# Second block's attention: index keys and queries projected first, index sums and selection beside the other projections, query roots as scale of the exponentials

## The reference

```python
    q = _rope(_rmsnorm(q, q_norm_g), positions)
    k = _rope(_rmsnorm(k, k_norm_g), positions)
    qi = _rope(qi, positions)
    ki = _rope(_layernorm(ki, idx_k_ln_g, idx_k_ln_b)[:, :, None, :], positions)[:, :, 0, :]
    ...
        s = jnp.einsum('bqhd,bsd->bqhs', qib, ki)
        score = jnp.einsum('bqhs,bqh->bqs', jax.nn.relu(s), wib).astype(jnp.float32)
        score = jnp.where(causal[None], score, -jnp.inf)
        _, sel = lax.top_k(score, topk)
        ...
        logits = jnp.einsum('bqgrd,bqkgd->bqgrk', qg, kg).astype(jnp.float32) * scale
        logits = jnp.where(sel_ok[:, :, None, None, :], logits, -1e30)
        p = jax.nn.softmax(logits, axis=-1).astype(vg.dtype)
```

## Time and profile before

| | us |
|---|---|
| median of 3 runs | 1908.45 (1906.66 to 1910.44) |
| the profiled execution, its own time | 1910.37 |
| its span, first to last instruction | 1908.6 |
| TensorE busy in the span | 1756.0 (92%) |
| VectorE busy | 1068.7 (56%) |
| ScalarE busy | 734.9 (39%) |
| GpSimd busy, 12 instructions | 12.0 (1%) |

### The profile page before, as it was taken

One profiled execution on the slowest core, in us unless ns is written; L12 is line 12 of the kernel. 1 busy time (PEld: TensorE's weight loads), 2 busy tenths in 40 slices (PEclk: granted clock), 3 DMA queues, 4 the chain that ended last, 5 costly groups with the idle time before them and its releaser, 6 DMA issues.

```text
span 1908.6 us, 22987 instructions
## 1 busy us (share of the span) xinstructions
PE 1756.0 (92%) x7616; PEld 1352.9 (71%) x7616; DVE 1068.7 (56%) x2153; ACT 734.9 (39%) x1406; POOL 12.0 (1%) x12
## 2 busy tenths in 40 slices
PE   5998999999979876676989999999899989999999
PEld 4777767777868753233668888888688868888887
DVE  7787676664465446884365656446645453333334
ACT  4455666652432213444344332223322344332222
POOL 0110000000000000000000000000000000000000
PEclk9999999999989985687989999999899989999999
DMA  5442444343312110000125555435233313333333
GB/s 220 154 162 62 152 139 149 133 147 117 95 56 67 56 55 1 1 1 1 55 78 198 180 209 184 144 117 180 67 101 97 99 57 97 100 99 99 90 101 107
DMA packets 55813, 201.67 MB, mean 106 GB/s; under 512 B 6192, under 2 KB 6320, under 8 KB 55600
## 3 DMA queue, kind: packets, MB, share of 16 engines
q1 hardware_dynamic: 55728, 200.57, 31.7%
HBM read 198.44 MB, written 2.10 MB: 105 GB/s over the span
## 4 chain that ended last, share of the span: by engine, by line
PE 82%; DVE 13%; ACT 3%; issue 2%; DMA 0%; DVEq 0%; ACTq 0%
PE bank L432 24%; PE bank L433 23%; PE bank L434 23%; PE bank L543 2%; PE bank L514 2%; PE bank L533 2%; DVE G L1202 1%; DVE SB L1331 1%; DVE SB L1355 1%; DVE WORK L1610 1%; PE bank L669 1%; PE bank L476 1%; DVE SM L1609 1%; DVE H_lo L1196 1%; DVE W_lo L1132 1%
## 5 line engine op out<-in xcount | busy, mean ns | idle before, releaser
L432 PE MATMUL bank<-H_hi,W_hi 128*128 128x512 f32 x1416 | 572.7, 404 | 24.8 <-DVE H_lo L1196 16.0
L433 PE MATMUL bank<-H_lo,W_hi 128*128 128x512 f32 x1416 | 554.9, 392 | 0.0
L434 PE MATMUL bank<-H_hi,W_lo 128*128 128x512 f32 x1416 | 554.8, 392 | 0.0
L1132 DVE TENSOR_TENSOR W_lo<-RAW,W_hi 128x512 fp32r<-128x512 f32 x538 | 349.5, 689 | 194.8 <-ACT W_hi L731 179.9
L731 ACT CAST W_hi<-RAW 128x512 fp32r<-128x512 f32 x538 | 312.6, 618 | 237.2 <-PE bank L434 214.3
L432 PEld LDWEIGHTS bank<-H_hi,W_hi 128*128 128x128 f32 x1416 | 267.4, 189 | 117.8 <-issue 44.0
L433 PEld LDWEIGHTS bank<-H_lo,W_hi 128*128 128x128 f32 x1416 | 268.1, 189 | 57.9 <-issue 5.8
L434 PEld LDWEIGHTS bank<-H_hi,W_lo 128*128 128x128 f32 x1416 | 267.7, 189 | 56.9
L434 PE MATMUL bank<-A_hi,W_lo 128*128 128x512 f32 x352 | 136.9, 389 | 0.0
L433 PE MATMUL bank<-A_lo,W_hi 128*128 128x512 f32 x352 | 136.9, 389 | 0.0
L432 PE MATMUL bank<-A_hi,W_hi 128*128 128x512 f32 x352 | 136.9, 389 | 0.0
(11 more groups left out here) (228 smaller groups left out, 1911.6 us busy)
## 6 DMA issues: line engine op xcount, KB each, us to landing
RAW<-weights SPq DMA_DIRECT2D x269, 512.0 KB, 3.6
AW<-ada SPq DMA_DIRECT2D x100, 512.0 KB, 3.6
X<-x_t SPq DMA_DIRECT2D x4, 512.0 KB, 5.9
y_t<-X SPq DMA_DIRECT2D x8, 256.0 KB, 2.0
LW<-lru_w SPq DMA_DIRECT2D x1, 1024.0 KB, 12.7
CROW<-crow SPq DMA_DIRECT2D x1, 512.0 KB, 10.7
ROPE<-rope SPq DMA_DIRECT2D x1, 512.0 KB, 13.5
CS<-constants SPq DMA_DIRECT2D x1, 386.5 KB, 8.4
```

The lines of the kernel that those rows point to most:

```text
L432: pe.matmul(dst, wh, ch(hi, k), start=(k == 0), stop=False)
L433: pe.matmul(dst, wh, ch(lo, k), start=False, stop=False)
L434: mm = pe.matmul(dst, wl, ch(hi, k), start=False, stop=(k == chunks - 1))
L1132: dve.tensor_tensor(W_lo[:, w], RAW[:, c:c + HALF], W_hi[:, w], ALU.subtract).then_inc(lo_done, 1)
```

## The change

The projections come in another order: index keys and weights first, then the four tiles of index queries, two of keys, two of values, eight of queries. The index products (`index`) go between the matmuls of the last key tile (n = 1), the value tiles (n = 2) and the first query tile (n = 3), with `RL` grown to five buffers, and for n = 1 two heads share one. Selection gets a list of rounds: seven ahead of the loop over query tiles, 23 in it (`ROUNDS_Q`), 18 in the attention steps (`ROUNDS_S`). Of the queries and keys only the raw tile times the gain goes into the turning; the mean squares by head are put into columns, `-0.5` power on GpSimd and one correction step on VectorE (`root_step`) make the roots, and for queries the root is no longer multiplied in: it is the `scale` operand of the exponentials and is in the negated maximum (`minus_max`). Keys are scaled after turning (`keys_normed`). Index keys are centred with a matmul by `centre`. In attention the logits rotate through three banks, three of four heads' scores are made one step ahead, and the orders of ScalarE and VectorE in a step are others.

```diff
+            def index(n, k):
+                if k % 2 == 0:
+                    return
+                chunk = k // 2
+                if n == 1 and chunk == 0:
+                    pe.wait_ge(wi_done, 2)
+                    pe.wait_ge(ki_done, 1)
+                if n == 1:
+                    pe.wait_ge(rope_done, 10 + chunk + 1)
+                for h in (2 * chunk, 2 * chunk + 1):
+                    u = IDX_UNIT(n, h)
+                    if u >= 2 and (n > 1 or chunk % 2 == 0):
+                        pe.wait_ge(relu_done, u - 1)
+                    rows, w = slice(64 * (h % 2), 64 * (h % 2) + 64), (n + 1) * P
+                    at_col = (chunk % 2) * w if n == 1 else 0
+                    mm = pe.matmul(ps[(5, 7)[h % 2]][:, at_col:at_col + w],
+                                   QI[rows, chunk * S + n * P:chunk * S + (n + 1) * P],
+                                   KI[rows, 0:w], start=True, stop=True)
+                    if n > 1 or chunk % 2 == 1:
+                        mm.then_inc(idx_mm, 1)
...
+            def in_k1(k):
+                if k == 2:
+                    pe.wait_ge(head_sq, 1)
+                    pe.wait_ge(krinv, 1)
+                    head_columns(ch(SQ, 0), 8, 4).then_inc(kcol_mm, 1)
+                if k == 3:
+                    rot2(4)
+                index(1, k)
...
+            def in_q(c):
+                def body(k):
+                    if c == 0:
+                        index(3, k)
...
-                              KI[rows, 0:(n + 1) * P], start=True, stop=True).then_inc(idx_mm, 1)
-                    m += 1
-            pe.wait_ge(relu_done, 24)
+                        if k == 2:
...
+            def query_columns(c):
+                pe.wait_ge(head_sq, 3 + c)
+                if c == 0:
+                    pe.wait_ge(krinv, 3)
+                head_columns(ch(SQ, c % 2), 24 + 8 * c if c < 4 else 8 * c, 4 if c < 4 else 6).then_inc(qcol_mm, 1)
...
+            pe.wait_ge(kd_done, 2)
+            pe.wait_ge(relu_done, IDX_UNITS)
+            qk(16, (0, 1))
+            query_columns(7)
+            rot2(13)
+            pe.wait_ge(rope_done, 10 + 13)
+            qk(16, (2, 3))
+            qk(17, (0, 1, 2))
...
             for s in range(16, 32):
                 if s < 31:
-                    qk(s + 1, (2, 3))
+                    qk(s + 1, (3,))
+                if s < 30:
+                    qk(s + 2, (0,))
                 turn_probs(s)
                 if s < 30:
-                    qk(s + 2, (0, 1))
+                    qk(s + 2, (1, 2))
...
+                        act.activation(SB[:, a:a + w], SB[:, a:a + w], ACT.Exp, bias=SM[:, m + 4 + h:m + 5 + h],
+                                       scale=q_scale(n, 4 * g + h),
+                                       accum_out=SM[:, m + 8 + h:m + 9 + h]).then_inc(exp_done, 1)
...
+                    ins = act.mul(ch(QN, i % 3), ps[tile.bank][:], pr(gain))
...
+            for c in range(10, 17):
+                split_hi(Tile(T_QKV2 + c + 1))
+                head_out(c, c - 3, "q_g")
+            exps(16)
             for s in range(16, 32):
-                exps(s)
+                probs_out(s)
                 if s > 16:
                     heads_out(s - 1)
+                if s < 31:
+                    exps(s + 1)
+                if s > 16:
                     heads_hi(s - 1)
-                probs_out(s)
...
+            for i in range(5):
+                pool.wait_ge(head_var, i + 1)
+                if i < 3:
+                    v, r = VK[:, 24 * i:24 * i + 8], VK[:, 24 * i + 8:24 * i + 16]
+                else:
+                    c = 32 * (i - 3)
+                    v, r = VQ[:, 64 + c:96 + c], VQ[:, c:c + 32]
+                pool.tensor_tensor(r, v, HALF_NEG[:, 0:1].to_broadcast([P, 8 if i < 3 else 32]), ALU.pow).then_inc(head_pow, 1)
...
+            def index_sum(u):
+                n, heads = (1, IDX_PAIRS[u]) if u < 4 else ((2, (u - 4,)) if u < 12 else (3, (u - 12,)))
                 w = (n + 1) * P
                 dst = SCALL[:, (n - 1) * S:(n - 1) * S + w]
-                for h in range(8):
-                    dve.wait_ge(relu_done, m + 1)
-                    rl = RL[:, (m % 2) * S:(m % 2) * S + w]
+                dve.wait_ge(relu_done, u + 1)
+                for x, h in enumerate(heads):
+                    rl = RL[:, (u % NRL) * S + x * w:(u % NRL) * S + (x + 1) * w]
                     wcol = WI[:, n * 8 + h:n * 8 + h + 1]
...
+            for c in range(10, 17):
+                split_lo(Tile(T_QKV2 + c + 1))
+                if c == 14:
+                    query_variance(0)
+                rope2_out(6 + c - 10)
+                if c == 14:
+                    query_roots(0)
+                select(ROUNDS_Q[c - 10])
...
+            score(16, 0)
+            score(16, 1)
+            query_variance(1)
+            rope2_out(13)
+            query_roots(1)
+            score(16, 2)
+            score(16, 3)
+            minus_max(16)
+            for h in range(3):
...
             for s in range(16, 32):
-                g, n, _ = STEPS[s]
-                if n < NB - 1:
-                    select(n + 1, range(4 * g, 4 * g + 4))
+                normalise(s)
                 if s < 31:
-                    scores(s + 1)
-                normalise(s)
+                    score(s + 1, 3)
+                    minus_max(s + 1)
                 if s > 16:
                     y_out(s - 1)
+                if s < 26:
+                    select(ROUNDS_S[s - 16])
+                if s < 30:
+                    for h in range(3):
+                        score(s + 2, h)
             y_out(31)
...
+ROUNDS_Q = [4, 5, 3, 3, 2, 3, 3]
+ROUNDS_S = [1, 2, 2, 2, 2, 2, 2, 2, 2, 1]
```

589 lines of the change are left out of this document (364 added, 225 removed).

## The result

The changed kernel takes 1894.11 us (median of 4 runs, 1892.58 to 1896.38) against 1909.08 us for the kernel before on the same chip: ratio 0.9924, 95% interval 0.9907 to 0.9941. It is faster by 0.8%, not by the 2.1% of the forecast, and lies outside the range of 1848 to 1890. The profiled execution has a span of 1892.9 us (before 1908.6).

What follows compares the result with a forecast made beforehand. TensorE sets the pace nearly everywhere but starves in the 50.8 us index chain and the attention steps. 1910.37 - 44.8 (front) + 2.7 (steps) + 1.4 (last step) = 1869.7 us, 1868 against the median; range 1848 to 1890.

Steps and rivals of the forecast that it cites:

- GpSimd's power: Projections and tail: power of 8 or 32 columns expected hidden behind a 2.3 us turn; 0 to 3 us, taken as 0.
- the scale from a column: 60 exponentials of the attention steps: 0 to 0.08 us each, 0 to 5 us in all, taken as 0.
- TensorE's work in the projections: Second block's projections: tiles, sums by head, spreads, full-width products and index products summed to 135.3 us.
- the discount of 5.1 us: Attention steps: three intervals at four key blocks taken with transposes at full clock, 2.0 us each, 5.1 us less.
- TensorE's end of the projections, 701: Projections from 558.3 us: 135.3 us of work, 4.5 idle and 3 of waiting for VectorE put TensorE's end at 701.
- The tail, 12 us: Between TensorE's end at 701 and first transposes near 713: VectorE ends at 705, then 7.5 us through the division.
- The steps, 160.5 us: First to last transposes: each step one chain without overlap, 165.6 less 5.1 us, a loss of 2.7 against 157.75.
- (b): Attention steps: TensorE keeps full clock in all, chain 149.9 instead of 160.5, time 1857; chance 0.20 for 1845 to 1860.
- (c): Projections: VectorE starves TensorE, each of eight query tiles 2 us longer, 16 us lost, 1884; chance 0.18 for 1880 to 1900.
- (d): Query tiles: gaps drop TensorE to half clock, 7.35 us a tile becomes 14.7, 1927 with all eight; chance 0.03.
- (e): Projections: a slow first power on GpSimd; at 6 us it costs 1 to 3 us, 1870; chance 0.03.
- (f): First projection tiles: the 50.8 us come back as waits, so nothing is won, near 1905; chance 0.03.

Runs made afterwards that it cites:

- e1_sub_late: Changed kernel with VectorE's subtraction `y_out(s - 1)` moved behind the selection and the three scores of s + 2 in the attention steps: 1841.09 us, ratio 0.9649.
- e7_sub_later_pieces: Changed kernel with query powers in pieces of 8 columns and `y_out(s - 1)` a full step later, behind the division of s + 1: 1823.59 us, ratio 0.9549.
- e3: Changed kernel with the query variances' power in eight pieces of 8 columns instead of two of 32: 1886.21 us, ratio 0.9872.
- e6: Changed kernel with 21 of the 23 selection rounds left out of the seven query tiles: 1881.89 us, ratio 0.9851.
- e11: Kernel with powers in pieces and `y_out` a step later (1823.6 us), with eight rounds moved from query tiles back into the steps: 1828.39 us.

## Why the prediction was wrong, step by step

The profiled execution took 1894.7 us, 25.0 more than the 1869.7 of the sum: 15.3 ahead of the first transposes, 8.8 in the steps, 0.2 in the last step, 0.7 behind. The steps of the prediction that failed are terms of its sum: GpSimd's power, taken at 0 and worth some 6.6 us; the scale from a column, taken at 0 and worth 5.6; TensorE's work in the projections, 135.3 us and measured 139.7; and the discount of 5.1 us for transposes at full clock, of which 3.0 did not come. Another 1.7 us of the front is scatter, and some 2.6 stay undivided between idle time in the first tiles and VectorE's lateness.

**What bounds it** was right: the front was won by putting its parts into queues that had room, and TensorE starved in the steps.

**TensorE's end of the projections, 701, came at 710.64.** Start 1.7 later, scatter (in the thirteen traces it lies between 558.1 and 560.1). Busy 139.7 us instead of 135.3, 4.4 off. Idle 11.0 instead of 7.5, 3.5 off. The busy time went wrong in the term that looked safest, 15 tiles of 5.47: their 360 matmuls kept TensorE busy 90.1 us and not 82.1, mostly because 12 of them fell in two short stretches at 1.2 GHz and those directly behind another product or a wait took some 0.11 us more than their neighbours. The other products took less than forecast, the index products 11.3 us and not 13.3, which hid half of that. The index products at full clock were right in the main: the clock of the stretches is 0.93 to 0.98.

**The tail, 12 us, took 17.9.** Here and in the idle time just named the failing step is the cost of GpSimd's power. I wrote "I take 0" with an upper bound of 1.5 us from products of 512 columns. In the changed kernel it took 1.6 to 2.0 us at 8 columns and 5.79 at 32. A bound taken from another operation, with other arithmetic for each element, was none. By the traces it cost some 6.6 us, beyond the 0 to 3 of the prediction: 3.0 of them lie in the projections, where TensorE waits for weight halves, and 3.6 in the tail. The other part is VectorE's lateness: I had put it 4 us behind TensorE, and it came to its first score only at 716.78, 6.1 behind. The prediction's own sign for this came, first transposes after 725 us: the starts of the query tiles lie 7.3 to 8.7 us apart, and once 10.8 (692.32 to 703.13), where the power's wait falls.

**The steps, 160.5 us, took 169.26.** The mechanism was right, part by part: the chain without overlap, its order, and `y_out` behind `heads_hi` behind the exponentials. Two terms were mis-sized. Exponentials 33.5, measured 39.1 (12.8, 11.1, 9.4, 5.8 by width): I had taken 0 of a stated 0 to 0.08 us for the scale, for which no row was given, and it is 0.09. And the discount of 5.1 for full clock at four key blocks: the three intervals' transposes took 3.67, 1.97 and 2.48 us, 8.1 and not 6.0, and those of the steps before 23.2, so 31.3 where 28.3 was forecast. With these two, the prediction's sum becomes 160.5 + 5.6 + 3.0 = 169.1. The rest of the sum held: laid out interval by interval, all other terms together were forecast at 98.7 us and took 98.9. The intervals are those of the forecast too: 10.2 to 11.1 us with one key block behind the first of 4.9 (near 10 expected), and 12.7, 11.2 and 9.7 with four (10.7 to 12.4 expected).

```profile
864.18 3.67 PE L551 MATMUL bank<-CS,SB 128*128 128x128 f32 x16 [0.62 <-DVE SB L1496]
...
876.89 1.97 PE L551 MATMUL bank<-CS,SB 128*128 128x128 f32 x16 [1.29 <-DVE SB L1496]
```

These rows also refute the reason I gave: an idle gap of 0.62 us ahead of the burst and half clock all the same, and in the next step twice the gap and full clock. The gap just ahead does not tell the clock.

The Trainium skill, "ScalarE: Activation LUTs", section "What ACT_TABLE_LOAD costs", says that each operand of an activation that is a column and not an immediate adds about 93 ns. The trace agrees (801 against 709 ns). An estimate by that page would have been 5.6 us for sixty calls, so the price was to be had beforehand.

**The last step** was forecast at +1.4 and took +1.6.

**Rivals.** (b), full clock in all steps, did not come (0.72), but the runs that shortened the wait came near it: 0.89 over the steps in e1_sub_late and 0.91 in e7_sub_later_pieces. The Trainium skill, "TensorE: Matmul & The Clock Gate", section "HAM oscillation — how this bites in real kernels", says that bursts with waits between them each start cold, and that a loop without those waits keeps the array warm. Three of the four stretches of e1_sub_late agree (0.92, 1.00 and 1.00, where the changed kernel's matching stretches have 0.71, 0.78 and 0.84); the first, with one key block, stayed at 0.63. The result lies in the interval of (c), 1880 to 1900, by another mechanism: GpSimd's power, the scale, the half clock and the longer tiles. (d), (e) and (f) didn't come: the query tiles ran at 0.98, the first power was no slower (1.64) than the later ones of its size, and 29.5 us were won ahead of the first transposes.

**The range.** I had named both unknown prices (0 to 5 for the scale, 0 to 3 for the power) and chosen the low end of each. At their upper ends the forecast would have been 1876. The misses all went one way, and the upper end of 1890 left 22 us above the forecast for costs that came to 26.

## What to carry to other kernels

When work leaves an engine's queue, follow the queue again with what is left: a short instruction that waits for another engine's late one holds everything behind it, and here it turned three engines into one chain, at a price of 53 us for 0.43 us of work. A wait is best put where its releaser is long done (`y_out` a step later), and whether work is free beside it can be tested by leaving the work out under either order. Price each new operand form and each operation on GpSimd by a row of the same operation, or carry the upper end.

## What was not expected of the hardware

A power with a column as exponent on GpSimd takes 5.42 or 5.79 us for 32 columns, and 1.63 to 2.17 us for 8, so some 0.16 us for each further column. The two values go with what VectorE does: in four traces (the changed kernel, e3, e6, e11) the power takes some 0.37 us more wherever a product of 512 columns is already under way on VectorE when it starts, and the short value where VectorE's next such product starts 0.4 us or more behind it. No run changes that alone, so it is seen but not shown as the cause. A scale from a column costs an exponential 0.09 us whatever its width (93 ns at 128 columns, 92 at 512). TensorE's transposes ran at the lower clock, 1.2 GHz, behind an idle gap of 0.62 us and at 2.4 GHz behind one of 1.29 us in the next step.
